# Reordering the attention schedule of layer 0 in a two-layer hybrid encoder

## The chip, the core and the metric

The kernel runs on one core of one Trainium2 chip. The metric is device time in microseconds (us) of one execution. Its engines work side by side, each through its own program in order, and wait for one another by semaphores: TensorE (PE) multiplies, VectorE (DVE), ScalarE (ACT) and GpSimd (POOL) do the elementwise work, SyncE (SP) issues most of the DMAs.

## What is computed

Two transformer layers over 1024 tokens of width 1024, in float32. The change touches only the first one up to its output projection.

```python
x = x + even_mixer(rmsnorm(x, a0_norm), a0_w_in, a0_w_out, a0_rpb)
x = x + swiglu(rmsnorm(x, f0_norm), f0_w_gate, f0_w_up, f0_w_down)
x = x + odd_mixer(rmsnorm(x, a1_norm), a1_w_qkv, ...)
x = x + swiglu(rmsnorm(x, f1_norm), ...)
return rmsnorm(x, final_norm)

def even_mixer(h, w_in, w_out, rpb):
    proj = h @ w_in                                  # 1024 x 3072
    qa, ka, va, qb, kb, vb = split(proj)             # 8 heads of 64 each
    ya = dilated_mixture_attention(qa, ka, va)       # windows 128, 512, 2048
    yb = neighborhood_attention(qb, kb, vb, rpb)     # 8 x 16 neighbourhood on a 16 x 64 grid
    return concat(ya, yb) @ w_out
```

## The kernel before

**Numbers.** Each float32 operand is split into a high part (a copy rounded to fp32r, on ACT) and a low part (the difference, on DVE or POOL). A product is three matmuls: high by high, high by low, low by high. A tile of 128 columns of the projection over 512 tokens is 8 chunks of three, so 24 matmuls; the code calls it a fill. `fill(P, k, a, b)` runs matmuls a to b of tile k of head pair P. Tiles 0 and 1 are the value, 2 and 3 the key, 4 and 5 the query, each for one half of the tokens.

**Pairs and steps.** Layer 0 has 8 head pairs: P = 0 to 3 are the dilated kind A, 4 to 7 the neighbourhood kind B. Each has 8 steps n, one for 128 queries. PE in step n runs qk (scores) of step n + 1, on even n the first PV (values by weights) of the two steps before, the turn (transposes) of head m = 0 of step n, a part of a fill of the next pair (`FILLS_AB`, `FILLS_TURN`, `FILLS_B`), value transposes `tv`, the second PV, the turn of m = 1, and a second part of a fill. The lists of fills are written out by hand; what a fill does in a step is cover for the chains of the other engines. Pair 7 has no next pair, so from its step 2 on there are no fills.

**Chains.** qk(n + 1) -> `ttr` on DVE (bias and minimum, lines 1508 and 1514) -> `exp` on ACT (lines 907 and 912) -> turn -> `hi` on ACT (line 942) -> `lo` on DVE (line 1589) -> PV -> `y_copy` on ACT (line 988) -> `y_add` on DVE (line 1596). In kind B, steps 2 to 5 have five blocks of keys; such a turn uses both T banks, and waits for the low part of the turn before it. Steps 0, 1, 6 and 7 have four. qk(n + 1) waits for both exps of step n. A projected tile is scaled by `evac` on DVE (lines 1476 and 1479), gets its high part by `kq_high` on ACT and its low part by `kq_low` on POOL (line 725). Values go through `tv` (line 2112), `vhi` (line 935) and `vlo` (line 1492), all by one bank.

**Weights.** SP loads a strip of weights in two halves (`raw`) when the low part of the strip before it is done; `w_split` on ACT and DVE splits it.

**Start.** `first_norm` on ACT and DVE splits x by chunks j and token halves h (`high`, line 820; `low`, line 1385) and squares it for the norm. PE starts with tiles 2, 3, 4 and most of 5 of pair 0, then sums the squares (line 2036), finishes tile 5, spreads the reciprocal root over the partitions (line 2043), and goes on with tiles 0 and 1, with qk(0, 0) between.

**Pair 7.** Here ACT and DVE also split the outputs of the earlier pairs for the output projection: `y_high` (line 1039) and `y_low` (line 1714), one chunk a step. The two PVs of a step use two banks, 6 and 7.

Of the kernel before, what the change touches and what calls it, by code (L numbers as in the profile page):

```python
# [80 lines left out]
def build(nc, x_in, wstrips, wdown, gains, subln, lams, ali_a, ali_c, tab_b, out):  # L81
# [207 lines left out]
    S = {}  # L289
# [73 lines left out]
    def t_count(P, n, m, kind):  # L363
# [10 lines left out]
    BETWEEN_AB = {1: [(1, 1, 9, 17)], 3: [(1, 3, 0, 8)]}  # L374
# [5 lines left out]
    FILLS_TURN = [([(1, 2, 8, 12)], [(1, 2, 12, 16)]), ([(1, 2, 16, 20)], [(1, 2, 20, 24)])]  # L380
    FILLS_TURN += [([(1, k, a, a + 6)], [(1, k, a + 6, a + 12)]) for k in (3, 4) for a in (0, 12)]
# [6 lines left out]
    def fills_at(P, n):  # L388

        parts = FILLS_AB[n] if P < 3 else FILLS_TURN[n] if P == 3 else FILLS_B[n] if P < 8 else FILLS_LATE[n]  # L390
        if P == 2 and n == NQ - 1:
            return [parts[0], [(2, 2, 0, 8)]]
        known = [(0, late(P)), (1, P % 8 < 7), (2, P < 2)]
        return [[p for p in part if (p[0], True) in known] for part in parts]
# [68 lines left out]
    def pv_bank(P, n, m):  # L463
        return FILL_BANK if P == 7 and m else PV_BANK
# [8 lines left out]
    def sync_program(e):  # L473
# [70 lines left out]
        def attention(layer):  # L544
# [3 lines left out]
            if layer:  # L548
                e.wait_ge(S["hrstd_done"], 2)
            else:  # L550
                raw(w0 + 3, layer)
                e.wait_ge(S["prstd_done"], 1)
            bias(P0, 0, kind_of(P0))
            if layer:
                raw(w0 + 3, layer)
            else:
                raw(w0 + 4, layer)
# [127 lines left out]
        raw(1, 0)  # L685
        e.dma_start(LV[:, :, :], lams.partition_broadcast(128)).then_inc(S["small_full"], 16)
        e.dma_start(SUBG[:, 0:1], subln).then_inc(S["small_full"], 16)
        attention(0)
# [108 lines left out]
    def act_program(e):  # L797
# [15 lines left out]
        def first_norm():  # L813
# [25 lines left out]
            for j in range(KC):  # L839
                high(j, 1)  # L840
            w_high(1, 0)
            w_high(1, 1)
            for j in range(KC):
# [7 lines left out]
            w_split(3, 1, 0, ("fill_done", 4))  # L851
# [189 lines left out]
        def begin(layer):  # L1041
# [10 lines left out]
            if layer == 0:  # L1052
                e.wait_ge(S["lam_ready"], 2)
                e.activation(NEGLAM[:, 0:2], NEGLAM[:, 2:4], ACT.Exp).then_inc(S["lam_ready"], 1)
            for m in range(2):
                exp(P0, 0, m, kind)

        def attention_mixed():
            begin(0)
            for P, n, after, last, more in order(0):  # L1060
# [8 lines left out]
                hi(P, n, 0, kind)  # L1069
# [4 lines left out]
                if after:  # L1074
                    exp(*after, 0, kind_of(after[0]))
                for v in middle(P, n):
# [4 lines left out]
                if after and (kind == "A" or P == 7):  # L1081
# [4 lines left out]
                if after and kind == "B" and P < 7:  # L1086
                    exp(*after, 1, kind_of(after[0]))
                if P == 7 and n in Y_AT:
                    y_high(0, Y_ORDER[0][Y_AT[n]])
# [268 lines left out]
    def dve_program(e):  # L1358
# [22 lines left out]
        def first_norm():  # L1381
# [18 lines left out]
            for j in range(KC):  # L1400
                low(j, 1)
            w_low(1, 0)
            w_low(1, 1)
            for j in range(1, KC):
# [10 lines left out]
            w_split(3, 1)  # L1415
# [197 lines left out]
        def begin(layer):  # L1613
# [13 lines left out]
            if layer == 0:  # L1627
                evac(P0, 0, FIRST_BANKS[4])
# [7 lines left out]
        def attention_mixed():  # L1636
            begin(0)
            for P, n, after, last, more in order(0):
# [9 lines left out]
                if kind == "A" or n < NQ - 1:  # L1648
                    lo(P, n, 0, kind)
                for v in middle(P, n):  # L1650
                    evac(*v)
                if kind == "B" and n == NQ - 1:
                    lo(P, n, 0, kind)
                if P == 7 and n - 1 in Y_AT:
                    y_low(0, Y_ORDER[0][Y_AT[n - 1]], Y_AT[n - 1])
# [15 lines left out]
            y_low(0, Y_ORDER[0][5], 5)  # L1671
# [354 lines left out]
    def pe_program(e):  # L2026
# [182 lines left out]
        def pv(P, n, m):  # L2209
# [6 lines left out]
            if P == 7 and n > 1:  # L2216
                e.wait_ge(S["y_done"], u)
            elif bank == PV_BANK:
# [43 lines left out]
        def begin(layer):  # L2262
            P0 = 8 * layer
            if layer == 0:
                for k in range(2, 5):
                    fill(P0, k, 0, 24, layer, prep=0, bank=FIRST_BANKS[k - 2])
                fill(P0, 5, 0, 18, layer, prep=0, bank=FIRST_BANKS[3])
                e.wait_ge(S["padd"], KC - 1)
                sums(ACCP, SSQ_BANK, "pssq_done")
                fill(P0, 5, 18, 24, layer, prep=0, bank=FIRST_BANKS[3])  # L2270
                e.wait_ge(S["prinv_done"], 1)
                spread(RT[:, 0, :], SSQ_BANK, "pspread_done")
                fill(P0, 0, 0, 24, layer, bank=FIRST_BANKS[4])
                fill(P0, 1, 0, 6, layer, bank=FIRST_BANKS[5])
                qk(P0, 0)
                fill(P0, 1, 6, 24, layer, bank=FIRST_BANKS[5])
# [392 lines left out]
```

## Time and profile before

| | us |
|---|---|
| three runs | 2716.58, 2716.70, 2718.95 |
| median | 2716.7 |
| the profiled execution, its time | 2718.95 |
| its span, first to last instruction | 2716.4 |
| outside the span | 2.55 |
| PE busy | 2655.5 |
| layer 0 up to the end of its attention, within the span | about 0 to 563 |

The profile is of one execution. Its time is that of the third run, 2.3 above the median. PE's matmuls overlap in the records, so the spacing of their starts says more than their durations. Idle time of an engine counts only where PE waits for it.

### The profile page before, as it was taken

The page shows a single profiled execution, that of the slowest core. Times are in us where ns is not written, and L with a number is a line of the kernel's source. Part 1 is how long each engine was busy: PE and PEld are TensorE (multiplying, and loading weights), DVE is VectorE, ACT ScalarE, POOL GpSimd, SP SyncE. Part 2 cuts the span into 40 slices and gives each one's busy share as a digit, 9 for nine tenths or more (in the row PEclk, how much of TensorE's full clock was granted, in tenths as well). Part 3 has the DMA queues.
Part 4 walks back from the last instruction along what each step waited for, and adds up shares of the span by engine and source line. Part 5 has one row for each costly group of instructions (what it writes and reads, how often), then busy time and mean ns, then how long its engine had stood idle before and what let it go on. Part 6 is the DMA issues. An engine that isn't in the chain of part 4 may idle for free.

```text
span 2716.4 us, 37391 instructions
## 1 busy us (share of the span) xinstructions
PE 2655.5 (98%) x13531; PEld 2162.6 (80%) x13531; DVE 1783.3 (66%) x2919; ACT 1116.0 (41%) x1998; POOL 142.5 (5%) x142
## 2 busy tenths in 40 slices
PE   8999999899999999999999999999999999999998
PEld 6888777688788888888777777778887888888886
DVE  5555655655666666666677777777556666666665
ACT  5555545534223322322445555555343233232333
POOL 0001022400000000000000000000000000000001
PEclk9999999999999999999999999998999999999999
DMA  3123243421111111111311111112211111111112
GB/s 121 57 58 81 66 117 110 146 101 54 51 47 55 51 58 46 50 51 54 112 44 46 46 47 46 46 47 82 84 51 55 47 47 55 50 58 46 51 47 77
DMA packets 101724, 173.73 MB, mean 64 GB/s; under 512 B 27296, under 2 KB 36944, under 8 KB 100048
## 3 DMA queue, kind: packets, MB, share of 16 engines
q1 hardware_dynamic: 90560, 162.26, 18.8%
q10 hardware_dynamic: 11024, 9.60, 1.4%
q8 instruction: 89, 1.46, 0.2%
q14 instruction: 51, 0.42, 0.0%
HBM read 151.74 MB, written 20.08 MB: 63 GB/s over the span
## 4 chain that ended last, share of the span: by engine, by line
PE 90%; ACT 3%; DVE 2%; issue 2%; DMA 1%; SPq 1%; POOL 1%; ACTq 0%; POOLq 0%; DVEq 0%
PE PS L2029 19%; PE PS L2031 19%; PE PS L2030 18%; PE PS L2099 16%; PE PS L2180 5%; PE PS L2249 4%; PE PS L2205 3%; ACT EC L912 1%; PE PS L2196 1%; PE PS L2226 1%; PE PS L2036 1%; PE PS L2112 1%; PE PS L2165 1%; PE PS L2230 1%; PE PS L2052 0%
## 5 line engine op out<-in xcount | busy, mean ns | idle before, releaser
L2099 PE MATMUL PS<-HH,WS 128*128 128x512 f32 x1536 | 523.3, 404 | 11.6 <-DVE HL L1385 8.2
L1168 ACT ACTIVATE WS<-WR 128x512 fp32r<-128x512 f32 x254 | 159.3, 629 | 459.7 <-PE PS L2031 318.4
L2099 PEld LDWEIGHTS PS<-HH,WS 128*128 128x128 f32 x1536 | 287.7, 189 | 70.3 <-DVE WS L1391 7.5
L2099 PE MATMUL PS<-HL,WS 128*128 128x512 f32 x768 | 302.3, 394 | 0.0
L1830 DVE TENSOR_TENSOR X<-PS,X 128x512 f32<-128x512 f32 x352 | 232.9, 685 | 80.4 <-PE PS L2031 78.5
L2029 PE MATMUL PS<-AH,WS 128*128 128x512 f32 x704 | 280.4, 398 | 3.1 <-issue 1.8
L2031 PE MATMUL PS<-AH,WS 128*128 128x512 f32 x704 | 278.8, 396 | 0.0
L2030 PE MATMUL PS<-AL,WS 128*128 128x512 f32 x704 | 278.4, 395 | 0.0
L2029 PE MATMUL PS<-TH,WS 128*128 128x512 f32 x640 | 251.6, 393 | 1.1 <-DVE WS L1772 1.1
L2031 PE MATMUL PS<-TH,WS 128*128 128x512 f32 x640 | 249.9, 391 | 0.0
L2030 PE MATMUL PS<-TL,WS 128*128 128x512 f32 x640 | 248.8, 389 | 0.0
L1772 DVE TENSOR_TENSOR WS<-WR,WS 128x512 fp32r<-128x512 f32 x254 | 174.7, 689 | 106.4 <-ACT WS L1168 102.7
L2029 PE MATMUL PS<-FH,WS 128*128 128x512 f32 x608 | 241.1, 397 | 1.8 <-DVE X L1750 1.8
L2031 PE MATMUL PS<-FH,WS 128*128 128x512 f32 x608 | 240.3, 395 | 0.0
L2030 PE MATMUL PS<-FL,WS 128*128 128x512 f32 x608 | 240.0, 395 | 0.0
L1514 DVE CUSTOM_DVE_ANT_0 PS<-PS,BIASC 128x1024 f32<-128x1024 f32 x128 | 154.3, 1247 | 34.4 <-PE PS L2180 33.2
L2099 PEld LDWEIGHTS PS<-HL,WS 128*128 128x128 f32 x768 | 145.7, 190 | 24.8
L2029 PEld LDWEIGHTS PS<-AH,WS 128*128 128x128 f32 x704 | 132.5, 188 | 35.7 <-issue 2.6
L2180 PE MATMUL PS<-KS,QS 64*128 64x512 f32 (+1 forms) x1056 | 144.9, 404 | 15.8 <-ACT EC L912 11.0
L2031 PEld LDWEIGHTS PS<-AH,WS 128*128 128x128 f32 x704 | 132.3, 188 | 32.7
L2030 PEld LDWEIGHTS PS<-AL,WS 128*128 128x128 f32 x704 | 132.4, 188 | 31.3
L2180 PEld LDWEIGHTS PS<-KS,QS 64*128 64x128 f32 x1056 | 96.4, 189 | 59.3 <-issue 44.8
(248 smaller groups left out, 4633.8 us busy)
## 6 DMA issues: line engine op xcount, KB each, us to landing
WR<-wstrips SPq DMA_DIRECT2D x304, 256.0 KB, 2.7
DR<-wdown SPq DMA_DIRECT2D x88, 256.0 KB, 2.6
BIASC<-ali_c SPq DMA_DIRECT2D x8, 960.0 KB, 6.5
BIAS<-tab_b SPq DMA_DIRECT2D x4, 1536.0 KB, 8.0
Y<-y_scratch SPq DMA_DIRECT2D x12, 512.0 KB, 7.0
BIAS<-ali_a SPq DMA_DIRECT2D x4, 1152.0 KB, 7.4
ya_scratch<-YS ACTq DMA_DIRECT2D x32, 128.0 KB, 2.4
MA<-a_scratch SPq DMA_DIRECT2D x16, 256.0 KB, 5.3
```

What stands on the lines that cost most here:

```text
L912: e.activation(e_tile(kind, m, n, P)[:, 0:128 * nk], banks(S_BANK[m], 2)[:, 0:128 * nk], ACT.Exp, scale=-1.0, bias=ST[:, n % 2, m:m + 1], ...
L1168: e.activation(WS[:, slot, 0, :], src, ACT.Copy).then_inc(S["w_hi"], 1)
L1514: e.tensor_tensor_reduce(out=s, in0=s, in1=(table if kind == "C" else table[:, m, :])[:, c:c + 128 * nk], scale=-1.0 if kind == "B" else 1 ...
L1772: e.tensor_tensor(WS[:, slot, 1, :], src, f(WS[:, slot, 0, :]), ALU.subtract).then_inc(S["w_lo"], 1)
L1830: e.tensor_tensor(xs, PS[:, D_BANK + at % 4, :], xs, ALU.add).then_inc(S["d_free"], 1)
L2029: e.matmul(ps, wh, xh, start=start, stop=False, skip_group_check=on)
L2030: e.matmul(ps, wh, xl, start=False, stop=False, skip_group_check=on)
L2031: return e.matmul(ps, wl, xh, start=False, stop=stop, skip_group_check=on)
L2099: last = e.matmul(ps, wt, xt, start=g == 0, stop=g == 23)
L2180: last = e.matmul(PS[:, S_BANK[m] + c // 4, 0:wd], QS[r, a, q], KS[r, P % 2, b, k], start=i == 0, stop=i == 2)
L2205: last = e.transpose(PS[:, bank + k // 4, 128 * (k % 4):128 * (k % 4) + 128], src[:, 128 * k:128 * k + 128], IDENT[:, :])
L2249: last = e.matmul(PS[:, bank, lo_:hi_], v, p, start=i == 0, stop=i == len(todo) - 1)
```

## The change

All edits reorder work or waits in the start and in the eight head pairs of layer 0. The number of matmuls and of elementwise operations stays.

- Strip 1 is split after the first four chunks of the second token half, and its load goes behind two small loads.
- Tile 5 of pair 0 is finished, and tile 0 begun, before the sums; the spread comes 18 matmuls later, qk(0, 0) stands 16 matmuls after the spread instead of 30.
- Strip 3 is loaded after the bias table of pair 0 and split after pair 0's query and key tiles.
- In step 3 of pairs 0 to 2, three matmuls go from before the second `tv` to behind it. Eight matmuls of tile (4, 2) go from the last step of pair 2 to the first two of pair 3.
- ACT: in kind B, `hi(n, 0)` comes after `exp(n+1, 0)` on even steps, and `exp(n+1, 1)` comes before `y_copy` and `hi(n, 1)`; in pair 7 `y_high` comes before `exp(n+1, 1)`.
- DVE: `lo(n, 0)` of the last step of kind B comes before the evacuation; in pair 7 `y_low` comes in the step of its `y_high`, before the second `y_add` and `lo(n, 1)`.
- PE: in pair 7 both PVs of a step use bank 6 but for the very last one, and wait for the `y_add` before.

```diff
-                ([(1, 2, 0, 7)], [(1, 2, 7, 14)]), ([(1, 2, 14, 24)], [(1, 3, 8, 10)]),
+                ([(1, 2, 0, 7)], [(1, 2, 7, 14)]), ([(1, 2, 14, 24)], [(1, 3, 5, 10)]),
-    BETWEEN_AB = {1: [(1, 1, 9, 17)], 3: [(1, 3, 0, 8)]}
+    BETWEEN_AB = {1: [(1, 1, 9, 17)], 3: [(1, 3, 0, 5)]}
-    FILLS_TURN = [([(1, 2, 8, 12)], [(1, 2, 12, 16)]), ([(1, 2, 16, 20)], [(1, 2, 20, 24)])]
-    FILLS_TURN += [([(1, k, a, a + 6)], [(1, k, a + 6, a + 12)]) for k in (3, 4) for a in (0, 12)]
+    FILLS_TURN = [([(1, k, a, a + 6)], [(1, k, a + 6, a + 12)]) for k in (2, 3, 4) for a in (0, 12)]
-        if P == 2 and n == NQ - 1:
-            return [parts[0], [(2, 2, 0, 8)]]
     def pv_bank(P, n, m):
-        return FILL_BANK if P == 7 and m else PV_BANK
+        return FILL_BANK if (P, n, m) == (7, NQ - 1, 1) else PV_BANK
...
             else:
-                raw(w0 + 3, layer)
                 e.wait_ge(S["prstd_done"], 1)
             bias(P0, 0, kind_of(P0))
-            if layer:
-                raw(w0 + 3, layer)
-            else:
+            raw(w0 + 3, layer)
+            if layer == 0:
                 raw(w0 + 4, layer)
...
-        raw(1, 0)
         e.dma_start(LV[:, :, :], lams.partition_broadcast(128)).then_inc(S["small_full"], 16)
         e.dma_start(SUBG[:, 0:1], subln).then_inc(S["small_full"], 16)
+        raw(1, 0)
...
-            for j in range(KC):
+            for j in range(4):
                 high(j, 1)
             w_high(1, 0)
             w_high(1, 1)
+            for j in range(4, KC):
+                high(j, 1)
...
-            w_split(3, 1, 0, ("fill_done", 4))
...
+            if layer == 0:
+                w_split(w0 + 3, 1, layer, ("fill_done", 6 * P0 + 4))
             for m in range(2):
                 exp(P0, 0, m, kind)
...
-                hi(P, n, 0, kind)
+                if kind == "A" or n % 2:
+                    hi(P, n, 0, kind)
...
                 if after:
                     exp(*after, 0, kind_of(after[0]))
+                if kind == "B" and n % 2 == 0:
+                    hi(P, n, 0, kind)
...
-                if after and (kind == "A" or P == 7):
+                if P == 7 and n in Y_AT:
+                    y_high(0, Y_ORDER[0][Y_AT[n]])
+                if after:
                     exp(*after, 1, kind_of(after[0]))
                 if last:
                     y_copy(*last, 1, kind_of(last[0]))
                 hi(P, n, 1, kind)
-                if after and kind == "B" and P < 7:
-                    exp(*after, 1, kind_of(after[0]))
-                if P == 7 and n in Y_AT:
-                    y_high(0, Y_ORDER[0][Y_AT[n]])
...
-                if kind == "A" or n < NQ - 1:
-                    lo(P, n, 0, kind)
+                lo(P, n, 0, kind)
+                if P == 7 and n in Y_AT:
+                    y_low(0, Y_ORDER[0][Y_AT[n]], Y_AT[n])
                 for v in middle(P, n):
                     evac(*v)
-                if kind == "B" and n == NQ - 1:
-                    lo(P, n, 0, kind)
-                if P == 7 and n - 1 in Y_AT:
-                    y_low(0, Y_ORDER[0][Y_AT[n - 1]], Y_AT[n - 1])
...
-            if P == 7 and n > 1:
-                e.wait_ge(S["y_done"], u)
-            elif bank == PV_BANK:
+            if bank == PV_BANK:
                 e.wait_ge(S["y_done"], 1 + u)
...
-                for k in range(2, 5):
+                for k in range(2, 6):
                     fill(P0, k, 0, 24, layer, prep=0, bank=FIRST_BANKS[k - 2])
-                fill(P0, 5, 0, 18, layer, prep=0, bank=FIRST_BANKS[3])
+                fill(P0, 0, 0, 6, layer, bank=FIRST_BANKS[4])
                 e.wait_ge(S["padd"], KC - 1)
                 sums(ACCP, SSQ_BANK, "pssq_done")
-                fill(P0, 5, 18, 24, layer, prep=0, bank=FIRST_BANKS[3])
+                fill(P0, 0, 6, 18, layer, bank=FIRST_BANKS[4])
                 e.wait_ge(S["prinv_done"], 1)
                 spread(RT[:, 0, :], SSQ_BANK, "pspread_done")
-                fill(P0, 0, 0, 24, layer, bank=FIRST_BANKS[4])
-                fill(P0, 1, 0, 6, layer, bank=FIRST_BANKS[5])
+                fill(P0, 0, 18, 24, layer, bank=FIRST_BANKS[4])
+                fill(P0, 1, 0, 10, layer, bank=FIRST_BANKS[5])
                 qk(P0, 0)
-                fill(P0, 1, 6, 24, layer, bank=FIRST_BANKS[5])
+                fill(P0, 1, 10, 24, layer, bank=FIRST_BANKS[5])
```

## Rows read from the trace of the kernel before

**Rows 1.** The page, busy us by engine (share of the span) and instructions.

```profile
PE 2655.5 (98%) x13531; PEld 2162.6 (80%) x13531; DVE 1783.3 (66%) x2919; ACT 1116.0 (41%) x1998; POOL 142.5 (5%) x142
```

**Rows 2.** PE's waits, whole span: releaser, us in total, times, longest.

```profile
PE PS L2205 <- DVE ATB L1589: 8.1, 6, 2.7
PE PS L2180 <- ACT E L912: 2.5, 8, 0.7
PE PS L2180 <- POOL QS L725: 2.0, 1, 2.0
```

**Rows 3.** Timeline at the start: start, duration, engine, line, operation, tiles, count.

```profile
11.29 7.64 ACT L820 ACTIVATE HH<-X,GAIN 128x512 fp32r<-128x512 f32 x12
...
17.14 0.61 PE L2099 MATMUL PS<-HH,WS 128*128 128x512 f32 x2
...
18.84 1.13 ACT L828 ACTIVATE WS<-WR 128x512 fp32r<-128x512 f32 x2
...
19.86 0.61 PE L2099 MATMUL PS<-HH,WS 128*128 128x512 f32 x2
```

**Rows 4.** DMA issues: strip 1 at 8.3 us, then strip 4 (us to landing last).

```profile
WR<-wstrips SPq DMA_DIRECT2D x1, 256.0 KB, 9.9
...
WR<-wstrips SPq DMA_DIRECT2D x2, 256.0 KB, 5.7
```

**Rows 5.** Timelines of POOL and PE up to the first qk.

```profile
42.49 2.54 POOL L725 TENSOR_TENSOR QS<-FS,QS 128x512 fp32r<-128x512 f32 x2
...
44.22 0.30 PE L2157 MATMUL PS<-KS,QS 64*128 64x64 f32 x2
```

**Rows 6.** Timeline, pair 0, step 3: value low part and the transpose behind it.

```profile
85.42 0.69 DVE L1492 TENSOR_TENSOR VS<-PS,VS 128x512 fp32r<-128x512 f32 x1 [1.19 <-ACT VS L935]
...
86.26 0.72 PE L2112 MATMUL PS<-IDENT,FS 128*128 128x128 f32 x4
```

**Rows 7.** Timeline around the end of pair 2 and the start of pair 3.

```profile
250.81 1.30 POOL L725 TENSOR_TENSOR QS<-FS,QS 128x512 fp32r<-128x512 f32 x1 [10.93 <-ACT QS L922]
...
252.16 0.62 PE L2155 MATMUL PS<-KS,QS 64*128 64x256 f32 x6
...
256.43 0.87 PE L2226 MATMUL PS<-ATA,VS 128*128 128x256 f32 x6
...
261.79 0.28 PE L2125 MATMUL PS<-IDENT,CA 128*32 128x128 f32 x1 [0.55 <-DVE CA L1534]
```

**Rows 8.** Timeline, pair 4, from y_copy of step 2 to the first turn of step 3.

```profile
329.14 0.38 ACT L988 ACTIVATE YS<-PS 64x256 f32<-64x256 f32 x1 [0.86 <-PE PS L2249]
...
329.69 0.71 ACT L942 ACTIVATE ATB<-PS 128x640 fp32r<-128x640 f32 x1 [0.16 <-PE PS L2205]
...
330.29 0.79 ACT L912 ACTIVATE E<-PS,ST 128x640 f32<-128x640 f32 x1
...
330.43 0.82 DVE L1589 TENSOR_TENSOR ATB<-PS,ATB 128x640 fp32r<-128x640 f32 x1 [0.46 <-ACT ATB L942]
...
331.31 1.24 PE L2180 MATMUL PS<-KS,QS 64*128 64x512 f32 x12 [0.27 <-ACT E L912]
...
332.48 0.77 PE L2205 MATMUL PS<-IDENT,E 128*128 128x128 f32 x5
```

**Rows 9.** Timeline, pair 7: y_add, y_high, and the first two y_low.

```profile
521.31 0.42 DVE L1596 TENSOR_TENSOR Y<-PS,YS 64x256 f32<-64x256 f32 x1 [1.13 <-ACT YS L988]
...
521.90 1.05 ACT L1039 ACTIVATE HH<-YE 128x1024 fp32r<-128x1024 f32 x1
...
525.26 1.28 DVE L1714 TENSOR_TENSOR HL<-YE,HH 128x1024 fp32r<-128x1024 f32 x1
...
533.33 3.12 DVE L1714 TENSOR_TENSOR HL<-YE,HH 128x1024 fp32r<-128x1024 f32 x1
```

**Rows 10.** Stretches of pair 7: us, engines' busy time, PE clock, DMA share, GB/s.

```profile
527.50:530.90 3.40, 3.40 (x22) 3.25 (x18) 2.76 (x4) 1.82 (x3) 3.40 (x4) 0.50 1.04 231
...
537.70:544.60 6.90, 4.95 (x20) 3.53 (x21) 5.00 (x11) 3.69 (x7) 3.27 (x2) 0.51 0.23 79
```

More of the change, by code:

```diff
@@ L1399, in first_norm @@
                 low(j, 0)
-            for j in range(KC):
+            for j in range(4):
                 low(j, 1)
@@ L1403, in first_norm @@
             w_low(1, 1)
+            for j in range(4, KC):
+                low(j, 1)
             for j in range(1, KC):
@@ L1414, in first_norm @@
             e.reciprocal(RT[:, 0, :], RT[:, 0, :]).then_inc(S["prinv_done"], 1)
-            w_split(3, 1)
         def root(N):
@@ L1627, in begin @@
             if layer == 0:
+                w_split(w0 + 3, 1)
                 evac(P0, 0, FIRST_BANKS[4])
@@ L1670, in attention_mixed @@
                     recip(P)
-            y_low(0, Y_ORDER[0][5], 5)
             for m in range(2):
```

## The prediction

> **What bounds the kernel now.** I read the page first, then the waits of TensorE, then the timeline around each place that the diff touches. The page says that PE is busy for 98% of the span [rows 1], at full clock nearly everywhere. So a step costs time when it leaves PE without a matmul that may run, and gains time only where PE waits now. The waits of PE in the changed layer are few [rows 2]: 8.1 us in six waits of a turn for the DVE's low part (all in pair 7), eight short waits of qk for an exp (2.5), one of 2.0 for POOL. That is some 13 us in all, the most the change could win back. Each edit moves work between or past these waits; none removes arithmetic. A matmul of 512 columns takes 0.227 us from start to start: twelve of them lie between 17.14 and 19.86 [rows 3].
>
> **The change part by part.** The diff falls into six places, all in layer 0. I follow each on the timeline, in the order of time.
>
> *First norm.* Now ACT runs twelve `high` of 0.64 us (11.29 to 18.93) and only then strip 1's two copies (1.13 together); DVE's low parts follow them one for one [rows 3]. Afterwards strip 1's copies stand before `high(4..7, 1)`. The order looks harmless until the load is read: strip 1's first half was issued at 8.35 and took 9.9 us to land [rows 4], 18.25, since the x loads fill the queues; now it is issued 0.9 us later, behind LV and SUBG. ACT has done `high(0..3, 1)` at 11.29 + 8 x 0.64 = 16.4 and stands until some 18.5, copies twice 0.6 to 19.65, and ends `high(4, 1)` at 20.3; DVE's low part of it is there at 21.1. PE wants it for the 13th matmul of tile 3, at 20.09 [rows 3]. After that DVE's low parts and PE's chunks of three matmuls advance alike. So +1.0 (0 if all lands early, 1.5 if late). The order of the squares has 2.6 us of slack, since the sums stand 12 matmuls later.
>
> *Sums, spread, first qk.* Eighteen more matmuls run before the spread (six of tile 5, six and twelve of tile 0): 18 x 0.227 = 4.1 us. The spread, RSTD and the POOL low parts all move by that: POOL's third, which `qk(0, 0)` needs, ends at 42.49 + 1.27 = 43.76 now, 47.85 then [rows 5]. Now PE runs 30 matmuls between spread and qk, which starts at 44.22 without a wait [rows 5]; afterwards 16, so it is there at 44.22 + 4.1 - 14 x 0.227 = 45.1 and waits 2.8 us. Qk starts at 47.9, and 14 matmuls follow instead of 18: 47.9 - 44.22 - 4 x 0.227 = +2.7. Strip 3's load, which is moved behind the spread and the bias load (SP's queue), is the next suspect: issued at 43.3, 5.7 us to land as strip 4's at that place has now [rows 4], 49.0; then two copies on ACT, two subtractions on DVE to 51.0, and only then `evac(0)`, the first bias sums and exps: the first turn may run at 53.9, and PE comes to it at 54.2. Hidden by 0.3 us; a load of 9.9 us instead would cost 3.8. I take +2.7, bounds 2.3 and 5.
>
> *Step 3 of pairs 0 to 2.* Three matmuls move from before the second value transpose to behind it. That transpose started at 86.26, at the end of eight matmuls; the low part that it waits for ended at 85.42 + 0.69 = 86.11 [rows 6], and wake-up takes 0.15 (the transpose at 86.26 could not have come sooner). So cover equals wait, and each matmul taken away is exposed: 3 x 0.227 = 0.68, three times, +2.0. I see nothing that takes it back; bounds 1.4 and 2.1.
>
> *Pair 2's last step.* Eight matmuls of tile (4, 2) leave it for pair 3. They hid the POOL low part of the last query tile: it ended at 250.81 + 1.30 = 252.11, and `qk(3, 1)` started at 252.16 [rows 7]. It still starts there, and the eight matmuls, 1.8 us, come on top. In pair 3 they fill two gaps: 0.3 before the second PV at 256.43 and 0.5 before the transpose of CA at 261.79 (0.55 idle) [rows 7]. +1.1, bounds 0.9 and 1.8.
>
> *The order on ACT in pairs 4 to 6.* Putting `exp(n+1, 1)` ahead of `hi(n, 1)` gives qk its exps earlier: the wait of 0.27 before 331.31 goes [rows 8]. But `hi(n, 0)` on even steps and `hi(n, 1)` now come 0.8 later. In steps 2 to 5 a tile of five blocks uses both T banks, so a turn waits for the low part before it. In step 2 the first delay holds the second turn by 0.4. Then exp 0.8, y_copy 0.4, hi 0.71 and lo 0.82 [rows 8] follow on one another where now hi and lo do: `lo(2, 1)` ends at 332.9 instead of 331.25, and the turn, at 332.48 now [rows 8], starts at 333.1. Step 4 gives +0.4 likewise. About +1.0 a pair. Pair 4's is swallowed: POOL is late there for a reason that hangs on SP and DMA, and PE has the 2.0 us wait [rows 2] as a cushion. 2 x 1.0, less 0.2 won in pair 4's step 0: +1.8. Bounds -1.9 (only the gains show) and +3.5. Moving `lo(7, 0)` ahead of the evacuation costs nothing: the fill that the evacuation waits for ends after it.
>
> *Pair 7.* Three edits meet where PE has no fills left as cover. `y_high`, 1.05 us [rows 9], goes ahead of `exp(n+1, 1)` in steps 2 to 6, which qk waits for. `y_low`, 1.28 alone but 3.12 at 533.33 beside POOL's long multiplications [rows 9], goes ahead of `lo(n, 1)`, which the next turn waits for. And the second PV takes the same bank as the first, so it waits for y_copy and y_add (0.38 [rows 8] and 0.42 [rows 9], with wake-ups 1.1) with one turn (0.5) as cover: 0.6, three times. Carrying the steps forward from qk(3) I get the next four qk later by 0.9, 1.9, 2.4 and 2.0 us: the delays overlap with the waits for `lo` that are there already. The second PV of step 6 makes it 2.7. I take +3.0; bounds 0 (the old waits hide all) and 8 (5 x 1.05 + 3 x 0.6 and 1 for the clock).
>
> The contention has a rule: the Trainium skill (GPSIMD Engine Reference, its table of properties) has POOL's SBUF interface shared with DVE instructions that read two SBUF inputs, which y_low does. By it, y_low in a POOL stretch waits in either order, and the place of the waits only moves. The row at 533.33 agrees.
>
> **Sum.** 1.0 + 2.7 + 2.0 + 1.1 + 1.8 + 3.0 = +11.6. On the profiled execution that is 2718.95 to 2730.6; it is 2.3 above the median, and I count from the median of 2716.7: **2728.3 us**, 0.43% slower. What a measurement tells from no change is about 0.2%, 5.4 us.
>
> **The rivals.**
> *The clock falls too.* In pair 7 PE ran at half clock for 3.4 us and again for 6.9 [rows 10], after short waits in quick succession; there its waits grow, and a new gap of 2.8 us stands before qk(0, 0). Against it: the 2.0 us wait before pair 5's qk has no such stretch behind it. Each further stretch like the first, with PE busy, costs half its length, 1.7. Two or three of them and pair 7's upper bound: +18 to +24, some 2737.
> The Trainium skill (TensorE: Matmul & The Clock Gate, section "Why this matters for your kernels") speaks against the change here: TensorE that idles between bursts goes back to half clock. By it this rival is the forecast; the row of the 2.0 us wait does not show it.
> *Waits that are there already swallow it.* As in pair 4: the delays of pairs 5 to 7 run into waits on `lo` and cost nothing, and strip 1 lands in time. Left are 2.7 + 2.0 + 0.5: +5, some 2721.5, within 0.2% or just beyond.
> *The change does nothing that counts:* all six places hidden. Against it are the exact hits of [rows 6, 7], with no slack at all. 2717, small chance.
> *Faster.* One mechanism: `y_low` in its own step leaves DVE before POOL's multiplications begin at 533, so no 3.12 us stop; the waits of pair 7 for `lo` (8.1) and both half-clock stretches (10.3, some 4 us of loss) go. That is -12, or with the +8.6 of the other places -3.5, 2713. It decides from the point where pair 7 wins more than 14. Against it: y_low then waits for y_high in its own step, and the third lies inside POOL's stretch.
>
> **How the numbers follow.** Forecast 0.70, clock 0.13, swallowed 0.10, nothing 0.04, faster 0.03. The forecast's own range is +6.5 to +17: 2723 to 2734. The range of 8 in 10 takes in part of both neighbours: 2721 to 2736. Slower by over 0.2% is the forecast, the clock and half of the swallowed, 0.88; within 0.2% 0.10; faster 0.02.
>
> **What would show it.** A PE wait before qk at 47 to 48 us on POOL's QS of near 2.8; a wait for HL near 20 of 1; three new waits of the second value transpose of 0.5 on DVE's VS near 86, 152 and 219, each later by the delay so far; a wait of 2.6 for POOL before pair 3's second qk; L2205-type waits on ATB of 0.4 to 0.6 in steps 3 and 5 of pairs 5 and 6; pair 4's wait on POOL smaller than 2.0; new waits of pair 7's PV on Y. Pair 7's stretch from qk(3) to its last PV must be longer by 3. Wrong would make it: pair 7 shorter, or strip 3's load landing past 49.4, or a clock at 0.5 outside pair 7.

## The result, and the profile after

The changed kernel takes **2731.64 us** (median of 5 executions, 2730.09 to 2738.84) against 2716.7 (5, 2716.58 to 2719.47): ratio 1.0061, interval 1.0049 to 1.0074, so 13 to 20 us slower. I had forecast 2728.3, 2721 to 2736, and slower with 0.88. The record holds 22 executions of the changed kernel, these five and the profiled one among them: 2730.1 to 2740.7, median 2734.1. The profiled execution took 2738.31 with a span of 2736.4; four others were above 2738 too. Its mean granted clock of 0.987 is the lowest of the 22 (the others 0.988 to 0.991), so it has more time at half clock (granted clock 0.50, the lower of its two levels) than the usual execution, and that matters below.

The page's row of busy times, and the waits of PE over the whole span (releaser, us in total, times, longest), answer to [rows 1, 2]:

```profile
PE 2665.0 (97%) x13531; PEld 2167.9 (79%) x13531; DVE 1779.4 (65%) x2919; ACT 1116.8 (41%) x1998; POOL 141.1 (5%) x142
...
PE PS L2202 <- DVE ATB L1589: 11.6, 16, 1.7
PE PS L2096 <- DVE HL L1384: 9.8, 3, 7.5
...
PE PS L2154 <- POOL QS L720: 2.7, 1, 2.7
PE PS L2109 <- DVE VS L1492: 2.5, 5, 0.6
PE PS L2152 <- POOL QS L720: 2.4, 1, 2.4
PE PS L2244 <- DVE Y L1596: 2.2, 3, 0.8
```

The matmuls are as many as before. Waits of the turn for ATB went from 8.1 us in 6, all in pair 7, to 11.6 in 16, of which eleven, together 5.4 us, are new ones in pairs 4 to 6; POOL's QS has two new waits of 2.7 and 2.4, VS and Y their small ones. PE's busy time rose by 9.5 us: the same matmuls ran longer, at half clock.

The start, timeline of the changed kernel (start, duration, engine, line, operation, tiles, count, idle before and what ended it):

```profile
18.82 1.26 ACT L823 ACTIVATE WS<-WR 128x512 fp32r<-128x512 f32 x2 [2.32 <-DMA WR<-wstrips]
...
21.53 0.50 PE L2096 MATMUL PS<-HH,WS 128*128 128x512 f32 x1 [1.43 <-DVE HL L1384]
...
48.15 2.49 POOL L720 TENSOR_TENSOR QS<-FS,QS 128x512 fp32r<-128x512 f32 x2
...
49.47 0.42 PE L2154 MATMUL PS<-KS,QS 64*128 64x64 f32 x2 [2.66 <-POOL QS L720]
...
50.49 1.19 ACT L799 ACTIVATE WS<-WR 128x512 fp32r<-128x512 f32 x2 [0.54 <-DMA WR<-wstrips]
```

ACT stands 2.32 us for strip 1, PE 1.43 for HL; the first qk waits 2.66 for POOL, where [rows 5] had none. Strip 3 lands about 50.4, 1.4 later than I had worked out. Then pair 0, step 3, and pair 3's second qk, the places of [rows 6, 7]:

```profile
93.12 0.72 PE L2109 MATMUL PS<-IDENT,FS 128*128 128x128 f32 x4 [0.54 <-DVE VS L1492]
...
259.69 1.26 POOL L720 TENSOR_TENSOR QS<-FS,QS 128x512 fp32r<-128x512 f32 x1 [10.93 <-ACT QS L918]
...
261.01 1.01 PE L2152 MATMUL PS<-KS,QS 64*128 64x256 f32 x6 [2.35 <-POOL QS L720]
```

And the stretches at half clock in layer 0 (engines' busy time with instructions, granted clock, DMA share, GB/s), beside [rows 10]:

```profile
49.10:55.90 6.80, 6.43 (x28) 5.34 (x29) 3.57 (x12) 3.93 (x12) 1.54 (x2) 0.50 0.44 155
260.70:267.50 6.80, 6.49 (x30) 5.88 (x31) 3.70 (x11) 2.37 (x7) 0.83 (x4) 0.50 0.00 0
540.60:547.40 6.80, 5.29 (x26) 4.63 (x26) 5.18 (x6) 4.24 (x8) 6.80 (x7) 0.50 1.05 233
554.30:561.10 6.80, 4.82 (x19) 3.39 (x20) 4.68 (x8) 3.69 (x7) 0.87 (x1) 0.50 0.25 80
```

The first two are new. Each begins some 0.4 us before the end of a wait of 2.4 to 2.7 us, and PE is busy through the rest of the stretch: it is work at half speed, not idle time.

A ledger by landmarks shows where the time went. I take the start of each qk in both traces; the difference is how late the changed kernel is there.

| stretch | late at its end, us | added | predicted |
|---|---|---|---|
| start to the second qk | 6.9 | 6.9 | 3.7 |
| pairs 0 to 2 | 8.9 | 2.0 | 2.0 |
| pair 2's last step, pair 3 | 11.6 | 2.7 | 1.1 |
| pairs 4 to 6 | 14.8 | 3.2 | 1.8 |
| pair 7, and on to the first products of the feed forward (699.23 before, 716.60 after) | 17.4 | 2.6 | 3.0 |
| the rest of the program, which the diff leaves alone | 20.0 | 2.6 | 0 |

A ledger from two executions takes in what is peculiar to either. In pairs 4 to 6 the kernel before ran, in its one profile, without a stretch at half clock that eight of the runs below have there; in those eight, where ACT's order is as before, the same row reads 1.6 to 2.4. Against such an execution the +3.2 of the changed kernel would be +0.8 to +1.6.

The last row is a stretch of 6.8 us at half clock at 1329.1, where the kernel before has 3.4 at 1312.6.

### The profile page after: what moved, and what is told of

The parts are those of the page before. It is cut to its first block, busy times and chain, and to the rows that moved or that the text cites. A ratio compares the mean times of both kernels' runs of the same rounds, so it can differ in the third digit from the quotient of the medians.

```text
span 2736.4 us, 37391 instructions
## 1 busy us (share of the span) xinstructions
PE 2665.0 (97%) x13531; PEld 2167.9 (79%) x13531; DVE 1779.4 (65%) x2919; ACT 1116.8 (41%) x1998; POOL 141.1 (5%) x142
## 3 DMA queue, kind: packets, MB, share of 16 engines
q8 instruction: 89, 1.46, 0.2%
## 4 chain that ended last, share of the span: by engine, by line
PE 88%; ACT 3%; DVE 3%; issue 3%; DMA 1%; SPq 1%; POOL 1%; ACTq 0%; POOLq 0%; DVEq 0%
PE PS L2026 19%; PE PS L2028 18%; PE PS L2027 18%; PE PS L2096 15%; PE PS L2177 4%; PE PS L2244 4%; PE PS L2202 3%; ACT EC L908 1%; PE PS L2221 1%; PE PS L2193 1%; PE PS L2162 1%; PE PS L2109 1%; PE PS L2225 1%; PE PS L2033 1%; PE PS L2049 1%
## 5 line engine op out<-in xcount | busy, mean ns | idle before, releaser
L908 ACT ACTIVATE EC<-PS,ST 128x1024 f32<-128x1024 f32 x128 | 141.1, 1113 | 3.5 <-DVE ST L1514 3.5
```

Of the source, the lines that this page charges most:

```text
L908: e.activation(e_tile(kind, m, n, P)[:, 0:128 * nk], banks(S_BANK[m], 2)[:, 0:128 * nk], ACT.Exp, scale=-1.0, bias=ST[:, n % 2, m:m + 1], ...
```

## The experiments

Each run but the last two is the kernel before with one part of the diff (in one of them doubled), timed beside it on the same chip; the kernel before took 2718.35, 2717.58 and 2718.21 us in the three groups, and its executions spread from 2712.2 to 2725.8. "Late" is the ledger's difference.

How much of a lateness is the edit's can be judged by the runs whose edit is elsewhere. Seven leave all of the start alone, and their second qk is late by -0.6 to +1.7 us; the four with +1.1 and more have a stretch of 3.4 us at half clock near 34 us, behind a wait of 0.16 to 1.16 us before the sums. Eight leave pair 7 alone, and it is longer by -0.2 to +1.0 us in seven of them, and by 5.2 in the eighth (ACT's order, below).

**The first norm**

```diff
-        raw(1, 0)
         e.dma_start(LV[:, :, :], lams.partition_broadcast(128)).then_inc(S["small_full"], 16)
         e.dma_start(SUBG[:, 0:1], subln).then_inc(S["small_full"], 16)
+        raw(1, 0)
...
-            for j in range(KC):
+            for j in range(4):
                 high(j, 1)
             w_high(1, 0)
             w_high(1, 1)
+            for j in range(4, KC):
+                high(j, 1)
```

> The kernel before with one part alone: strip 1 loaded behind LV and SUBG and split after four chunks of the second token half. My theory: ACT stands for the strip's load, and PE waits for HL once, near 20 us, for 1.4 (as the changed kernel's trace shows), and nothing takes it back: qk(0, 0) at 45.6 instead of 44.2, time +1.4 us. Rival (slack before the sums swallows it): the same wait, but qk(0, 0) at its old time, +0.

Measured 2719.36 us, ratio 1.0007 (0.9998 to 1.0016): +1.9 us, nothing that can be told from none. PE waits 0.94 for HL near 21 us, near the 1.0 of the prediction (I had expected the changed kernel's 1.4 here). The first qk is late by 3.87, at 48.1 where I had expected 45.6: PE also waits 0.63 before the sums, and some 1.7 (half of it, an estimate) is a stretch of 3.4 us at half clock at 36.3 that the kernel before did not have in its profile. Runs that leave the start alone have the same stretch, so it is not this edit's.

**PE's order at the start, and the same with a later qk**

```diff
-                for k in range(2, 5):
+                for k in range(2, 6):
...
-                fill(P0, 0, 0, 24, layer, bank=FIRST_BANKS[4])
-                fill(P0, 1, 0, 6, layer, bank=FIRST_BANKS[5])
+                fill(P0, 0, 18, 24, layer, bank=FIRST_BANKS[4])
+                fill(P0, 1, 0, 10, layer, bank=FIRST_BANKS[5])
                 qk(P0, 0)
-                fill(P0, 1, 6, 24, layer, bank=FIRST_BANKS[5])
+                fill(P0, 1, 10, 24, layer, bank=FIRST_BANKS[5])
```

> The kernel before with PE's new order alone: sums 12 and spread 18 matmuls later, qk(0, 0) 16 matmuls after the spread; strip 3 loaded and split where it was. Theory: a wait of 2.7 us before qk(0, 0) for POOL's QS; with it the clock falls to half behind that wait for 3.4 to 6.9 us while PE is busy, so +2.7 of wait and +1.7 to 2.7 of clock, together +4.4 to 5.4 at the second qk. Rival 1 (the wait alone): +2.7, clock stays at full. Rival 2 (strip 3's late load did the harm in the changed kernel): +0 to 1 here.

The second kernel has 22 in place of 10 in these fills, so qk(0, 0) stands after 28 matmuls.

> As the run before it, but qk(0, 0) stands 28 matmuls after the spread instead of 16, so that PE has work until POOL's part is there. Theory: POOL's third low part ends at 47.9 and PE comes at 47.9: wait 0 to 0.2 us, no half clock, the time within 0.5 us of the kernel before. If the sums and the spread themselves cost (rival: more matmuls before them make all later), the loss stays at 2 us or more.

Measured: 2719.59, ratio 1.0006 (0.9997 to 1.0015), and 2718.22, ratio 1.0000 (0.9990 to 1.0010). In the first, qk waits 2.67 for POOL, 3.4 us at half clock follow at 48.1, and the second qk is late by 3.05, where I had expected 4.4 to 5.4. From the first qk to the second it loses 1.5, as the stretch would have it. But in this execution the clock rose to full at 10.5 us and not at 15.5 as in the kernel before, PE was 1.1 us ahead by its twentieth matmul, and so the first qk is late by 2.50 where wait and order alone give 3.6. In the second there is no wait and no such stretch, and it is late by 0.51, of which 0.4 is there by the twentieth matmul, ahead of all that the edit moves. So the order itself costs nothing that shows; the wait and the stretch come with the qk that stands too early in it.

**Strip 3 late**

```diff
-                raw(w0 + 3, layer)
                 e.wait_ge(S["prstd_done"], 1)
             bias(P0, 0, kind_of(P0))
+            raw(w0 + 3, layer)
...
-            w_split(3, 1, 0, ("fill_done", 4))
...
+                w_split(w0 + 3, 1, layer, ("fill_done", 6 * P0 + 4))
```

> The kernel before with strip 3's load and split alone moved behind the bias load and the query and key tiles. Theory: hidden. The load is issued at 39.2, lands near 45, the split ends near 48 on DVE, the first bias sums start 48 to 49 instead of 46.1, the first turn may run at 50.9 and PE comes to it at 51.6: +0 to 0.4 us. Rival (a part of the loss at the start is this split): a new wait of PE at the first turn, +1 to 3 us.

Measured 2717.68, ratio 0.9997 (0.9988 to 1.0006); the second qk is late by 0.28. The first exp starts 4.1 us after the first qk, where the kernel before has 3.0, and the first turn does not wait for it. Hidden, as predicted.

**Six matmuls moved in step 3**, twice the diff's three:

```diff
-                ([(1, 2, 0, 7)], [(1, 2, 7, 14)]), ([(1, 2, 14, 24)], [(1, 3, 8, 10)]),
+                ([(1, 2, 0, 7)], [(1, 2, 7, 14)]), ([(1, 2, 14, 24)], [(1, 3, 2, 10)]),
...
-    BETWEEN_AB = {1: [(1, 1, 9, 17)], 3: [(1, 3, 0, 8)]}
+    BETWEEN_AB = {1: [(1, 1, 9, 17)], 3: [(1, 3, 0, 2)]}
```

> The kernel before with six matmuls (twice the change's three) moved behind the second value transpose in step 3 of pairs 0 to 2. Theory: cover equals wait, each matmul moved costs its 0.227 us: 6 x 0.227 = 1.36 a pair, waits of the transpose for VS of 1.2, time +4.1 us. Rival (PE makes it up in the next steps, where it also waits): +2 or less, the third qk behind it back at its distance.

Measured 2721.66, ratio 1.0013 (1.0004 to 1.0022), +3.5. PE's waits between 80 and 230 us:

```profile
PE PS L2112 <- DVE VS L1492: 3.7, 3, 1.2
```

Three waits of 1.2, and the lateness steps up by 1.38, 1.38 and 1.37: six times 0.227 is 1.36. The exchange is one for one, matmul by matmul.

**Pair 2's last step**

```diff
-    FILLS_TURN = [([(1, 2, 8, 12)], [(1, 2, 12, 16)]), ([(1, 2, 16, 20)], [(1, 2, 20, 24)])]
-    FILLS_TURN += [([(1, k, a, a + 6)], [(1, k, a + 6, a + 12)]) for k in (3, 4) for a in (0, 12)]
+    FILLS_TURN = [([(1, k, a, a + 6)], [(1, k, a + 6, a + 12)]) for k in (2, 3, 4) for a in (0, 12)]
...
-        if P == 2 and n == NQ - 1:
-            return [parts[0], [(2, 2, 0, 8)]]
```

> The kernel before with the eight matmuls of tile (4, 2) alone moved from pair 2's last step to pair 3. Theory: a wait of 2.4 us before qk(3, 1) for POOL, net +1.1 us by pair 3's fourth step at full clock; the clock may fall for up to 6.8 us behind it, then +2.8. Rival (the clock fell in the changed kernel for what came before, not for this gap): +1.1 in every run, clock at full near 250 to 257.

Measured 2719.49, ratio 1.0008 (0.9999 to 1.0017). The wait is there, but the clock stays up behind it (the last column but two):

```profile
253.19 0.62 PE L2152 MATMUL PS<-KS,QS 64*128 64x256 f32 x6 [2.35 <-POOL QS L722]
```

```profile
250.00:254.00 4.00, 1.65 (x16) 1.32 (x16) 1.38 (x2) 2.02 (x6) 1.84 (x4) 1.00 0.00 0
254.00:258.00 4.00, 4.00 (x30) 3.53 (x29) 2.95 (x10) 1.97 (x6) 0.00 (x0) 1.00 0.00 0
```

From the second to the fifth qk of pair 3 only 0.3 of lateness is added, where I had 1.1 at full clock. In the changed kernel the same wait is followed by 6.8 us at half clock and 2.8 is left.

**ACT's order in pairs 4 to 6, and exp alone.** The first kernel has both moves, for P < 7; the second only the last four lines, the exp:

```diff
-                hi(P, n, 0, kind)
+                if kind == "A" or n % 2 or P == 7:
+                    hi(P, n, 0, kind)
...
+                if kind == "B" and n % 2 == 0 and P < 7:
+                    hi(P, n, 0, kind)
...
-                if after and (kind == "A" or P == 7):
+                if after:
...
-                if after and kind == "B" and P < 7:
-                    exp(*after, 1, kind_of(after[0]))
```

> The kernel before with ACT's new order alone in pairs 4 to 6 (hi(n, 0) behind exp(n+1, 0) on even steps, exp(n+1, 1) ahead of y_copy and hi(n, 1)). The changed kernel's trace has from pair 4's first qk to pair 5's +0.7, then +0.9 and +1.5. Theory: the same here, +3.1 us, with pair 4's delay of 2.4 mostly swallowed by the wait for POOL. Rival: the loss there hung on the delays before it, +1 or less.

> As the run before it, but only exp(n+1, 1) ahead of y_copy and hi(n, 1); hi(n, 0) stays. Theory: qk's waits of 0.27 go, the second turn of steps 2 and 4 no longer waits; left is the next step's first turn, which waits for lo(n, 1), 0.4 in steps 3 and 5: +0.5 to 1.5 us in all. Rival (hi(n, 0)'s place did the whole harm): faster than before by 1 to 2 us.

Measured 2722.49, ratio 1.0013 (1.0004 to 1.0022), and 2720.63, ratio 1.0016 (1.0007 to 1.0025). The exp alone gives +0.1, +0.5 and +0.9 us in pairs 4, 5 and 6; both moves 0.0, +1.0 and +1.5. The median of the exp alone, +4.3 (1.9 to 6.8), is more than the 0.5 to 1.5 that I had expected; its profile is of the fastest of its eleven executions (2716.03), that of both moves of the slowest (2727.72), so what a usual execution of either spends is not shown. PE's wait for POOL before pair 5 is gone or down to 0.40 in these two: pair 4's delay is swallowed, as predicted. What I had not seen is a wait in step 6, in the changed kernel:

```profile
361.33 0.82 DVE L1589 TENSOR_TENSOR ATB<-PS,ATB 128x640 fp32r<-128x640 f32 x1 [0.31 <-ACT ATB L938]
362.07 0.68 DVE L1476 TENSOR_TENSOR FS<-PS,RSTD 128x512 f32<-128x512 f32 x1
362.30 0.74 PE L2202 MATMUL PS<-IDENT,E 128*128 128x128 f32 x5 [0.84 <-DVE ATB L1589]
```

The first turn of step 6 has four blocks, but the code lets it, too, wait for every low part before it, and that of step 5 is late.

**Pair 7: the PV bank alone, and the order of the Y split alone**

```diff
-        return FILL_BANK if P == 7 and m else PV_BANK
+        return FILL_BANK if (P, n, m) == (7, NQ - 1, 1) else PV_BANK
...
-            if P == 7 and n > 1:
-                e.wait_ge(S["y_done"], u)
-            elif bank == PV_BANK:
+            if bank == PV_BANK:
```

> The kernel before, with one part of the change: in pair 7 the second PV of a step takes the same bank as the first and waits for its y_add. By my theory the three second PVs that this touches wait for Y with one turn as cover, as in the changed kernel (0.83, 0.78 and 0.55 us there); the first of them has a qk and a step behind it with no fill. Ends 1 to 2 us later by the lateness of pair 7's last qk and PV, up to 1.8 more if a stretch of half clock is added or 3.5 less if one goes. Rival 1, the old waits hide it: PE waits for Y, and by as much less for the low parts (8.1 us before), net 0 to 0.4. Rival 2, the bank is all of pair 7's cost: +2.6, which is what the pair lost with all three edits.

```diff
+                if P == 7 and n in Y_AT:
+                    y_high(0, Y_ORDER[0][Y_AT[n]])
                 if after and (kind == "A" or P == 7):
...
-                if P == 7 and n - 1 in Y_AT:
-                    y_low(0, Y_ORDER[0][Y_AT[n - 1]], Y_AT[n - 1])
+                if P == 7 and n in Y_AT:
+                    y_low(0, Y_ORDER[0][Y_AT[n]], Y_AT[n])
```

> The kernel before, with the other part of pair 7's change: y_high ahead of the second exp of the next step, y_low ahead of the second low part of its own step; the PVs keep their two banks. By my theory a new wait of near 1 us before a qk for an exp and longer turn waits for low parts near 540 and 555: pair 7 longer by 1 to 2.5. If the order is all of pair 7's cost it is +2.6 and the PV bank's run shows 0. Rival, the low part that leaves its step early is out of the way of the low part of the next step: pair 7 shorter by 0.5 to 3, with the half clock stretch of 6.8 us near 538 gone. In both cases the y_low near POOL's long multiplications takes some 3 us, wherever it stands.

Measured: bank 2719.37, ratio 1.0006 (0.9996 to 1.0017), its pair 7 longer by 1.1, which is within the scatter of runs that leave pair 7 alone. PE's waits there do change: 3.8 us in three for Y, where there were none, and 2.6 less for the low parts. Order: 2722.56, ratio 1.0018 (1.0009 to 1.0027), pair 7 longer by 3.6, and three stretches at half clock of 17.0 us in all, where [rows 10] have 10.3. That is more than the 1 to 2.5 that I had expected. The order is the dearer of the two in medians and ledger, though the intervals overlap; the rival by which it shortens the pair is out.

**Another edit of pair 7**: POOL's scaling of Y in four pieces, y_low after the second low part.

```diff
-            e.tensor_tensor(Y[:, k, :], Y[:, k, :], YQ[:, k, :], ALU.mult).then_inc(S["ymul_done"], 1)
+            for c in range(4):
+                y = Y[:, k, 256 * c:256 * c + 256]
+                last = e.tensor_tensor(y, y, YQ[:, k, 256 * c:256 * c + 256], ALU.mult)
+            last.then_inc(S["ymul_done"], 1)
```

> The kernel before, with an edit that the change does not make: in pair 7 y_low comes after the second low part of its step in place of ahead of it, and POOL's multiplications that scale Y are done in four pieces of 256 columns each, so that a DVE operation on the same tile stream may come between them. If contention with POOL is what stretches y_low from 1.28 to 3.12 us, and that delays the low part and the turn, then the longest waits of pair 7 for a low part (2.7 us) shrink by 1 to 2 and the attention ends 1 to 4 us earlier (the upper end if a half clock stretch goes with them); the y_low itself stays slow, unless the pieces free the port, when it drops toward 1.5. Rival: y_low only moves, the low part after it is late all the same, and the end stays within 0.5 us; POOL's pieces cost it up to 1 us more in all, off the path.

Measured 2718.49, ratio 1.0003 (0.9994 to 1.0012): no gain. The longest wait for a low part fell from 2.7 to 1.6 us, as expected, but pair 7 did not get shorter: the rival holds. The y_low inside POOL's stretch is quick (DVE, then POOL):

```profile
540.21 1.46 DVE L1717 TENSOR_TENSOR HL<-YE,HH 128x1024 fp32r<-128x1024 f32 x1
```

```profile
535.72 9.27 POOL L785 TENSOR_TENSOR Y<-Y,YQ 128x256 f32<-128x256 f32 x12
```

It took 1.46 where [rows 9] have 3.12 beside whole multiplications, and POOL's twelve pieces took 9.3 us against 8.0 for three. PE now waits 2.6 for an exp instead. The Trainium skill (SBUF — State Buffer, "SBUF: two separate sides") says that the pair of ports which VectorE and GpSimd share is locked for a whole instruction by whichever starts first. The quick y_low between pieces agrees; the row at 539.84 of the next run does not agree as it stands, since the DVE operation there began first by its record and yet ended after both of POOL's.

**The changed kernel with a later first qk**

```diff
-                fill(P0, 1, 0, 10, layer, bank=FIRST_BANKS[5])
+                fill(P0, 1, 0, 22, layer, bank=FIRST_BANKS[5])
                 qk(P0, 0)
-                fill(P0, 1, 10, 24, layer, bank=FIRST_BANKS[5])
+                fill(P0, 1, 22, 24, layer, bank=FIRST_BANKS[5])
```

> The changed kernel itself, but with the first qk of pair 0 after 28 matmuls behind the spread in place of 16. If the gap of 2.7 us before it and the half clock stretch of 6.8 us that follows are what the start costs beyond the first norm, both go: the second qk is late by 1.5 to 2.5 us in place of 6.9, perhaps 0.9 comes back at the first turn, and the time is 3.5 to 5 us below that of the changed kernel, some 2727.5, ratio to the kernel before near 1.0045 in place of 1.0061. Rival: the clock falls a little later all the same, or the exps that now come 2.7 us later hold the first turns: then the gain is 0 to 1.5 us and the ratio stays at 1.0055 or more.

Measured 2733.33 (6 executions), ratio 1.0062 (1.0050 to 1.0074): the rival holds, and within the intervals (3.3 us either way for each kernel) nothing is gained. Its profile explains half of that. The wait and the stretch at half clock are gone, the second qk is late by 1.46, but the first turn then waits 1.94 for an exp. So 3.5 are left of 6.9, and at the start of pair 7 it is late by 9.9 against 14.8. There it gives the gain back (DVE and POOL, then PE):

```profile
539.84 6.10 DVE L1362 TENSOR_TENSOR WS<-WR,WS 128x512 fp32r<-128x512 f32 x1
540.60 4.79 POOL L778 TENSOR_TENSOR Y<-Y,YQ 128x1024 f32<-128x1024 f32 x2
```

```profile
548.55 2.79 PE L2244 MATMUL PS<-ATB,VS 128*128 128x256 f32 x12 [3.91 <-DVE Y L1596]
```

A low part of a weight of 512 columns, 0.65 us elsewhere (two in 1.29 at 51.15), took 6.10 while two of POOL's multiplications ran; behind it y_add was late, and PE waited 3.9. Pair 7 cost 6.7 us here against 2.6. The run of ACT's order has the same collision, although its edit leaves pair 7 alone; that profile lost 5.2 us there, and PE's longest wait was 5.8:

```profile
533.04 8.49 DVE L1364 TENSOR_TENSOR WS<-WR,WS 128x512 fp32r<-128x512 f32 x2 [0.64 <-ACT WS L804]
535.80 5.19 POOL L783 TENSOR_TENSOR Y<-Y,YQ 128x1024 f32<-128x1024 f32 x2
...
544.27 1.08 PE L2206 MATMUL PS<-IDENT,E 128*128 128x128 f32 x4 [5.83 <-DVE ATB L1590]
```

**Do the parts make up the whole?** By their ratios times 2717, step 3 at half: 1.9 + 1.6 - 0.8 + 1.8 + 2.2 + 3.5 + 1.6 + 4.9 = 16.7 us, against 16.6 for all together. Each has an interval of some 2.4 either way, so the sum of eight has 7; it says that no cost above some 7 us comes from two parts meeting, not more. One move of the diff stands in no part: `lo(n, 0)` of kind B's last step ahead of the evacuation. That it costs nothing, as predicted, was not tested.

## Why the prediction was right, and where its terms were off

**The direction** came from exact hits of cover against wait, and the waits stood where they were foretold: near 20, before the first qk, in step 3, before pair 3's second qk. **The size** is less well earned. The median is 3.3 us above the forecast, that of all 22 executions 5.8; what the sum left out is stretches at half clock behind the new waits, and some of its terms hit for other reasons than those given.

**First norm, +1.0.** Held: a wait of 1.43 near 20 where I had 1.0, inside its bounds, and 0.94 and 0.90 in two runs with the same edit; ACT waited for strip 1 as worked out, the copies starting at 18.82.

**Sums, spread, first qk, +2.7.** The wait of 2.66 came as worked out (2.8). With the first norm's, the term was too small in the profiled execution by 3.2 us: at the second qk 6.9 was lost, not 3.7. Some 2.5 of that was lost between the first qk and the second. What failed is the step that let PE go on at full speed after the wait; it ran at half clock for 6.8 us. The single part, with 3.4 us at half clock, was late by 3.05, near the +2.7 only because its clock had risen earlier at the very start, worth 1.1.

**Strip 3** landed at 50.4, past the 49.4 that I had named as the point where it would make me wrong, and yet cost nothing in the changed kernel. The exps start at 53.99, in time for a first turn at about 55.1 (in the last run they start at 53.96 and the turn that waits for them at 55.03); PE came to it at 58.42, and without the 2.5 us lost at half clock it would have come near 55.9 (an estimate), still 0.8 later. The load itself took 5.5 from its issue at 44.95, where I had 5.7; the point of 49.4 was set too early, since it left out that the first norm's wait delays the issue, qk(0, 0) and PE together. In the last run the exps were as late, but twelve matmuls had gone from behind the first qk to before it: PE reached the turn that much sooner and waited 1.94.

**Step 3 of pairs 0 to 2, +2.0.** 0.69, 0.69 and 0.67: 2.05. Doubled, it doubles. This is the term that is shown best.

**Pair 2's last step, +1.1.** 2.8 with 6.8 us at half clock, 0.3 without (the run alone). The wait of 2.35 held (2.6). The term lies between the two cases and hit neither. At full clock I had left out a third gap that the eight matmuls fill: in the kernel before, PE waits 0.51 for YS before the PV at 269.42, in the run alone it does not, and the lateness falls from 1.0 to 0.3 there. At half clock it was 2.8 all the same.

**ACT's order, +1.8.** Measured 3.2 in the changed kernel and 2.5 alone, both against the one execution of the kernel before that ran pair 5 without half clock; against the usual 1.6 to 2.4 it is +0.8 to +1.6 in the changed kernel and +0.1 to +1.0 alone. Within steps 1 to 5 the pairs lose 0.85, 0.86 and 0.78 each, near the +1.0 less 0.2 that I had. The step that failed is the list of turns that wait for all low parts: I took steps 2 to 5, and the first turn of step 6 waits as well, 0.84 a pair, of which part is given back at the pair's end. Pair 4's cushion worked: the wait of 2.0 for POOL was 0.40.

**Pair 7, +3.0.** 2.6 in the profile of the changed kernel, qk later by 0.8, 1.7, 2.8 and 1.9 against 0.9, 1.9, 2.4 and 2.0. But the two parts alone measure 1.6 and 4.9, with intervals of 2.4 to 2.8, and the last run's profile lost 6.7 there. Runs that leave the pair alone scatter by some 1 us. The single number was luck; "0 to 8" described it.

**The rival of the clock** I gave 0.13, on the ground that the wait of 2.0 us before pair 5 had no stretch at half clock behind it. That row was one execution. Nine profiles here have this wait at 2.0, the kernel before and eight of the runs above, and in the eight runs 3.4 us at half clock begin within 1.5 us of the wait's end; only the profile I had read escaped. Other short waits beside it do not tell them apart: three of the eight have, in the 20 us before, the same single wait of 0.27 as the kernel before. The five with 1.21, 0.40 or no wait have none. The wait and what follows in the run of strip 3, then a stretch as long in the kernel before:

```profile
367.06 1.17 PE L2178 MATMUL PS<-KS,QS 64*128 64x512 f32 x6 [2.00 <-POOL QS L723]
```

```profile
364.40:367.80 3.40, 1.40 (x9) 0.68 (x8) 2.68 (x4) 0.81 (x3) 2.94 (x5) 0.98 0.98 304
367.80:371.20 3.40, 3.40 (x12) 2.62 (x11) 1.41 (x4) 1.26 (x3) 0.28 (x2) 0.52 0.03 12
```

```profile
365.50:368.90 3.40, 3.40 (x20) 2.62 (x21) 1.41 (x4) 1.48 (x4) 0.63 (x3) 1.00 0.16 60
```

PE makes 12 matmuls in the second stretch, where the kernel before made 20. The direction of the Trainium skill's rule (TensorE: Matmul & The Clock Gate, "Why this matters for your kernels") was the better guide: TensorE that idles between bursts goes back to half clock. But that section warns of longer gaps than any here, so by its letter it did not speak for this rival, as the prediction had it; that 2.0 us can be enough is what these runs show. The change even takes one such stretch away, with the wait before pair 5. The profiled execution of after, 2738.3, is what I had worked out for this rival (some 2737), and five of the 22 are above 2738; the median is not. How much of the median's +15 is the clock is not settled: the profiled execution has some 4.5 to 5 us of it at the start and in pair 3 (an estimate: 6.9 where the waits alone give some 4.3, and 2.8 where they give 0.3 to 1.1), and it is itself 6.7 above the median at the lowest clock of all. The four others above 2738 had 0.989, as many a faster one. The runs have profiles of one execution each, so I cannot say how often the median one drops.

**The other rivals.** Waits that swallow it, 2721.5, is out, though pair 4's part of it was seen. *Faster* needed y_low to leave before POOL's multiplications, and pair 7 to win more than the rest loses. The first two y_low did leave before them; what then met POOL was the low part of a weight (two took 2.68 in the changed kernel, 3.45 in the run of the order alone, against 1.28 to 1.29 elsewhere), and the pair lost 2.6.

## What to carry to other kernels

A wait that is covered exactly, matmul for matmul, is a debt: take one matmul of cover away and it comes back, in full in step 3, while before pair 3 most of 2.35 us was won back in three gaps behind it. Price a new wait with what may follow it, the wait itself and as often as not half of a stretch at half clock; and never take "no drop here" from one execution. Before a ledger of two profiles is read, look which of the two has a stretch at half clock that the other lacks. Where POOL has long multiplications beside a chain of DVE, ask, whenever the two shift against each other, which instruction they will meet; it may be one that costs nothing, or one on which the next PV hangs.

## What was not expected of the hardware

- Waits as short as 2.0 us had half clock behind them in eight profiles of nine, 2.35 (the wait before pair 3's second qk) in two of three, 2.66 and 2.67 in two of two. At the start it came behind still shorter ones: of the six profiles with a wait of 0.16 to 1.16 us before the sums, five have a stretch at half clock that begins 1.8 to 2.9 us after it. A stretch of 3.4 near pair 5 costs 1.5 to 1.6 us from one qk to the next.
- A DVE instruction of 0.65 us took 6.10 beside two of POOL's of 2.4, although it had begun 0.76 before them; cut in four, POOL's pieces let a y_low through in 1.46.
- Executions of the same kernel before spread over 13 us (2712.2 to 2725.8), wider than any of the single parts is worth.
